# Decode states only read in the mixers and updated later on POOL; the loops over heads run one head ahead

## What is computed

```python
def step(carry, inp):                       # mLSTM, one chunk (decode: a chunk of 1)
    ...
    num = einsum('bhts,bshv->bthv', s, vc) + einsum('bht,bhvd,bthd->bthv', w_inter, cm, qc)
    den = jnp.sum(s, axis=-1) + w_inter * einsum('bhd,bthd->bht', nv, qc)
    ...
    cm_new = decay[..., None, None] * cm + einsum('bhs,bshv,bshd->bhvd', w_end, vc, kc)
    nv_new = decay[..., None] * nv + einsum('bhs,bshd->bhd', w_end, kc)

# SSD:       y = decay * cb @ x + exp(acum) * C h;   h_new = exp(acum_last) * h + w_end * x B^T
# retention: o = att @ v + w_inter * q s;            s_new = decay * s + w_end * k v^T
```

## Time and profile before

| | us |
|---|---|
| median of 3 runs | 2354.97 (2351.16 to 2358.28) |
| span of the profiled execution | 2355.1 |
| PE / DVE / ACT / POOL busy | 2187.6 / 1344.2 / 969.9 / 332.2 |
| mixers, layer 0 (first gate matmul to the squares) | 192.0 to 397.3 |
| mixers, layer 1 | 1045.5 to 1256.2 |

### The profile page before, as it was taken

One profiled execution on the slowest core, in us unless ns is written; L12 is line 12 of the kernel. 1 busy time (PEld: TensorE's weight loads), 2 busy tenths in 40 slices (PEclk: granted clock), 3 DMA queues, 4 the chain that ended last, 5 costly groups with the idle time before them and its releaser, 6 DMA issues.

```text
span 2355.1 us, 39779 instructions
## 1 busy us (share of the span) xinstructions
PE 2187.6 (93%) x16079; PEld 2027.9 (86%) x16079; DVE 1344.2 (57%) x2052; ACT 969.9 (41%) x1434; POOL 332.2 (14%) x344
## 2 busy tenths in 40 slices
PE   7998986999899999989887998899999999999997
PEld 6997765996589989988677994699999999999997
DVE  6446777541256566448676531456666666665665
ACT  4444212442155454452114441344455454454544
POOL 0872222000000004942221000000000000000000
PEclk9998888999999999998779999989999999999998
DMA  6552222454745444542222454535444544545543
GB/s 268 187 186 82 97 72 74 162 179 159 256 148 171 172 158 163 180 143 90 78 76 106 145 187 171 195 120 194 151 181 160 202 175 147 202 155 183 178 171 116
DMA packets 60747, 367.41 MB, mean 156 GB/s; under 512 B 7332, under 2 KB 7780, under 8 KB 28452
## 3 DMA queue, kind: packets, MB, share of 16 engines
q1 hardware_dynamic: 48708, 322.78, 38.8%
q0 software_dynamic: 11872, 42.28, 5.1%
HBM read 340.55 MB, written 24.48 MB: 155 GB/s over the span
## 4 chain that ended last, share of the span: by engine, by line
PE 86%; DVE 8%; ACT 3%; DMA 2%; issue 1%; SPq 0%; POOL 0%; DVEq 0%; ACTq 0%
PE ps L460 22%; PE ps L461 21%; PE ps L462 21%; PE ps L546 5%; PE ps L757 2%; PE ps L714 2%; PE ps L448 2%; PE ps L475 1%; DVE stream L1273 1%; DVE wL L309 1%; PE ps L478 1%; PE ps L738 1%; PE ps L725 1%; PE ps L477 1%; PE ps L476 1%
## 5 line engine op out<-in xcount | busy, mean ns | idle before, releaser
L309 DVE TENSOR_TENSOR wL<-ring,wH 128x1024 fp32r<-128x1024 f32 x591 | 730.2, 1237 | 508.9 <-ACT wH L303 506.7
L460 PE MATMUL ps<-hH,wH 128*128 128x264 f32 x2784 | 796.5, 286 | 19.7 <-issue 12.0
L461 PE MATMUL ps<-hL,wH 128*128 128x264 f32 x2784 | 792.4, 285 | 0.0
L462 PE MATMUL ps<-hH,wL 128*128 128x264 f32 x2784 | 791.8, 284 | 0.0
L303 ACT ACTIVATE wH<-ring 128x1024 fp32r<-128x1024 f32 x591 | 622.7, 1055 | 341.3 <-PE ps L462 265.6
L460 PEld LDWEIGHTS ps<-hH,wH 128*128 128x128 f32 x2784 | 528.2, 190 | 26.6 <-issue 22.8
L461 PEld LDWEIGHTS ps<-hL,wH 128*128 128x128 f32 x2784 | 528.4, 190 | 0.0
L462 PEld LDWEIGHTS ps<-hH,wL 128*128 128x128 f32 x2784 | 525.8, 189 | 0.0
L460 PE MATMUL ps<-projR,wH 128*128 128x264 f32 (+1 forms) x1520 | 437.7, 288 | 32.6 <-DVE projR L1353 17.3
L462 PE MATMUL ps<-projR,wL 128*128 128x264 f32 (+1 forms) x1520 | 436.7, 287 | 0.0
L461 PE MATMUL ps<-projR,wH 128*128 128x264 f32 (+1 forms) x1520 | 435.8, 287 | 0.0
(11 more groups left out here) (288 smaller groups left out, 2056.8 us busy)
## 6 DMA issues: line engine op xcount, KB each, us to landing
ring<-w_gu_dram SPq DMA_DIRECT2D x110, 1024.0 KB, 4.8
ring<-w_in_dram SPq DMA_DIRECT2D x58, 1024.0 KB, 4.7
ring<-w_down_dram SPq DMA_DIRECT2D x80, 704.0 KB, 4.1
stream<-states_dram POOLq DMA_DIRECT2D x32, 512.0 KB, 3.6
ring<-w_out_dram SPq DMA_DIRECT2D x16, 1024.0 KB, 4.7
o_states_dram<-stream POOLq DMA_DIRECT2D x32, 512.0 KB, 2.9
ring<-kc_dram SPq DMA_DIRECT2D x16, 1024.0 KB, 4.8
ring<-vc_dram SPq DMA_DIRECT2D x16, 1024.0 KB, 4.8
```

The lines of the kernel that those rows point to most:

```text
L309: dve.tensor_tensor(wL[:, buf * PIECE:(buf + 1) * PIECE], slot(s, half * PIECE, PIECE), f32(wH[:, buf * PIECE:(buf + 1) * PIECE]), ALU.sub ...
L460: pe.matmul(dst, wh, high(k0 + k), start=k0 + k == 0, stop=False)
L461: pe.matmul(dst, wh, low(k0 + k), start=False, stop=False)
L462: ins = pe.matmul(dst, wl, high(k0 + k), start=False, stop=k0 + k == k_all - 1)
```

## The change

1. **Reading.** The states are stored transposed (k x v instead of v x k, in the host's layout). `read_state(u)` on TensorE is eight matmuls with a sequence's 128x128 of the old state as weights and its q column as the one moving column; the 48 or so results of all units gather in PSUM. `spread`, `unit_half` and `decay` go. The terms with k.q come from one matmul with a block of ones (nkq), and y is finished for all heads of a kind in a few operations of 128x48 (behind mLSTM's first head, in `ssd_steps` behind the first retention head's weighing, and behind the last).
2. **Updating.** K and V (times their gates) of all units are kept in kU and vU. vU is transposed once (L671, ScalarE copies it to vT) and written to a small DRAM tensor `vrow`. When POOL has scattered the decode queries of cross attention it goes over the 16 units: load the old state again, load the unit's row of `vrow` broadcast to 128 partitions, multiply the state by its decay, the rows by k, add, write. One buffer for rows, two for states.
3. **One head ahead.** mS, mEM, mVK, mKW get two buffers (rVK, rKW in retention), the SSD tiles move to other space, products of SSD to bank 1 and 3. The loops run `a(h + 1)` before `d(h)` on TensorE, and the same on ACT and DVE.
4. **Moved.** All four rotations go ahead of the mLSTM heads. The gate activations (conv Silu, z, g, sigmoid) go from behind ACT's first two heads to ahead of them. K's scaling goes from ACT to DVE. The gate weights of layer 1 are loaded on SP behind the eighth weight block instead of at the start. `output_gate(0)` goes from unit 7 to behind unit 12.

```diff
+                def read_state(u):
+                    pe.wait_ge(state_in[u % STATE_SLOTS], 16 * state_count(l, u))
+                    S, q = state(u), unit_q(u)
+                    for b in range(NB):
+                        ins = pe.matmul(bank(u // (NH + SP), u * NB + b, 1), S[:, b * P:(b + 1) * P], q[:, b:b + 1], start=True, stop=True)
+                    ins.then_inc(dec_read, 1)
...
+                for u in range(NH):
+                    read_state(u)
+                    if u == 0:
+                        pe.wait_ge(k_scaled, l + 1)
+                    if u < RH:
+                        rotate(u)
+                pe.wait_ge(nq_ready, l + 1)
+                pe.matmul(bank(0, NQ, P), ones, nkq[:, 0:P], start=True, stop=True).then_inc(nden_ready, 1)
...
+                ml_a(0)
                 for h in range(NH):
-                    ml_a(h)
...
-                    spread(h, 0)
+                    if h + 1 < NH:
+                        ml_a(h + 1)
                     ml_d(h)
-                    spread(h, 1)
...
+                for j in range(SP):
+                    if j + 1 < SP:
+                        ssd_a(j + 1)
+                    read_state(NH + j)
+                    ssd_d(j)
+                    if j + 1 < SP:
+                        ssd_turn(j + 1)
+                pe.wait_ge(rows_ready, l + 1)
+                pe.transpose(bank(4, V_TURN, P), vU[:, :], ident).then_inc(rows_turned, 1)
...
                 for h in range(RH):
...
                     if h + 1 < RH:
+                        ret_a(h + 1)
+                    read_state(NH + SP + h)
+                    ret_d(h)
...
+                st(dve.tensor_scalar(proj[:, K_ML * NT:V_ML * NT], proj[:, K_ML * NT:V_ML * NT], P ** -0.5, None, ALU.mult))
...
+                for h in range(RH):
+                    rotate(h)
...
                 for u in range(UNITS):
-                    if u + 2 < UNITS:
-                        decay(u + 2)
-
-                    pool.wait_ge(dec_S, 2 * (l * UNITS + u + 1))
-                    pool.dma_start(t["o_states"][l, u], state(u)).then_inc(state_out[u % STATE_SLOTS], 16)
+                    pool.wait_ge(dec_read, l * UNITS + u + 1)
                     if u + STATE_SLOTS < UNITS:
-                        pool.wait_ge(state_out[u % STATE_SLOTS], 16 * state_count(l, u))
-                        pool.wait_ge(dec_read, 2 * (l * UNITS + u + 1))
                         load_state(l, u + STATE_SLOTS)
...
+                rows = stream[:, 2 * 1024:3 * 1024]
+                pool.wait_ge(rows_out, 16 * (l + 1))
+
+                def load_update(u):
+                    if u > 1:
+                        pool.wait_ge(state_out[u % 2], 16 * (l * UNITS // 2 + u // 2))
+                    pool.dma_start(stream[:, (u % 2) * 1024:(u % 2 + 1) * 1024], t["states"][l, u]).then_inc(upd_state[u % 2], 16)
...
+                for u in range(UNITS):
...
+                    if u + 1 < UNITS:
+                        load_update(u + 1)
...
+                        st(pool.tensor_tensor(S3, S3, dec.unsqueeze(2).to_broadcast([P, NB, P]), ALU.mult))
...
+                    pool.wait_ge(upd_rows, 16 * (l * UNITS + u + 1))
+                    st(pool.tensor_tensor(V3, V3, kU[:, u * NB:(u + 1) * NB].unsqueeze(2).to_broadcast([P, NB, P]), ALU.mult))
+                    st(pool.tensor_tensor(S, S, rows, ALU.add))
+                    if u + 1 < UNITS:
+                        load_rows(u + 1)
+                    pool.dma_start(t["o_states"][l, u], S).then_inc(state_out[u % 2], 16)
```

More of the change, by code:

```diff
@@ L1302, in _ @@
+                ml_weigh(0)
+                for h in range(NH):
+                    n, i = l * NH + h, h % 2
+                    if h + 1 < NH:
+                        ml_weigh(h + 1)
                     dve.wait_ge(ml_num, n + 1)
[L1303 removed]
+                    st(dve.scalar_tensor_tensor(out=mDN, in0=bank(6, SEQ, SEQ), scalar=-1.0, in1=mEM[i], op0=ALU.mult, op1=ALU.max))
@@ L1347, in _ @@
+                for h in range(RH):
+                    gamma = float(np.float32(1.0) - np.float32(2.0) ** np.float32(-5.0 - h))
+                    ins = dve.scalar_tensor_tensor(out=tile(proj, Q_R + h, SEQ, NB), in0=bank(1, 96 + h * NB, NB), scalar=gamma,
+                                                   in1=yK[:, h * NB:(h + 1) * NB], op0=ALU.mult, op1=ALU.add)
+                ins.then_inc(dec_y, 1)
                 dve.wait_ge(ret_h, (l + 1) * RH)
@@ L1591, in _ @@
+                pool.sem_inc(updated, 1)
                 pool.wait_ge(dma_out, 16 * OUTS * (l + 1))
+                for s in range(2):
+                    pool.wait_ge(state_out[s], 16 * (l + 1) * UNITS // 2)
 OUTS = 11
```

461 lines of the change are left out of this document (248 added, 213 removed).

## The result

The changed kernel takes 2405.7 us (median of 4 runs, 2399.2 to 2409.2) against 2356.1 (2351.2 to 2358.3) for the kernel before, timed beside it: a ratio of 1.0205 with a 95% interval of 1.0184 to 1.0226, slower. 2295 was forecast, 2215 to 2350 its range. The profiled execution spans 2407.0 us, 51.9 more than the one before.

A forecast was written before the change was run, and what follows sets the result against it. The tensor engine bounds nearly everything (86% of the chain that ended last). 2355.1 us, less 84 in the mixers, plus 24 for the update on POOL, gave 2295 us; range 2215 to 2350.

The forecast's parts named there:

- The share at half clock: Mixers: 40% of PE's work at half clock, so 78 - 0.4 x 91 = 42 us less a layer, 84 in all.
- its two ends: Mixers, per layer: 78 us less with PE wholly at full clock, 13 us more with it wholly at half clock.
- the prediction's own sum: Mixers of a layer at full clock: 12.6 + 40.5 + 55 + 19.5 = 127.6 us against 205.3.
- The sizes at full clock: Mixers: a read 1.5 us, mLSTM head 5.9, SSD pair 8.6, retention head 4.2; heads start 12.6 us later.
- The update: POOL from cross attention into the FFN: 11.5 us a unit, costing 12 us a layer (0 to 44), 24 in all.
- the dearer alternative: FFN: by the exclusive-lock rule each weight split could wait a whole POOL multiply, costing 10 us a layer, not 2.
- Half clock through both mixers: Rival: narrow reads and gates leave PE busy but slow in the mixers; +26 + 24, 2405 us; 10%.
- The dear lock: Rival: cross attention +20, norm +6, FFN +10, DMA +8, 44 us a layer; 2359 us, no change; 8%.
- Full clock throughout: Rival: PE waits less and holds full clock in the mixers, the whole 156 us come; 2223 us; 22%.
- Late states: Rival: PE waits for the last three of six state reads, about 3 us each, 10 a layer; 2315 us; 12%.
- The signs named for the second rival: Mixers: granted clock under 0.65 points to half clock; mixers not falling under 190 us make the forecast wrong.
- the other sign of being wrong: Forecast wrong if the stretch from 545 to 670 us grows by more than 25.

The follow-up runs named there:

- e11: Changed kernel with gate and step matmuls reading 128 rows instead of 6 or 12 (zeros added), e2 timed again in rounds: 2270.8 us, ratio 0.9641.
- e2: Changed kernel with gate and step matmuls reading 128 rows instead of 6 or 12 (added rows zeros): 2274.6 us in a single run.
- e14: Changed kernel with 128 rows in the SSD gates and steps only, mLSTM gates keeping 6 rows: 2295.8 us in a single run.
- e5: Kernel before the change, broadcasts kept, with its gate and step matmuls reading 128 rows instead of 6 or 12: 2305.0 us, ratio 0.9779.
- e4: Changed kernel with 96 unused 128x128 matmuls a layer added, at the gates and behind the first six reads: 2407.4 us in a single run.
- e10: Changed kernel with 128-row gates and update begun in the FFN, plus the six mLSTM reads moved inside the heads: 2276.4 us, ratio 0.9644.
- e9: Changed kernel with 128-row gates and the update begun only after the layer's first FFN gate-up tile: 2286.4 us, ratio 0.9698.
- e16: Changed kernel with 128-row gates, reads in mLSTM heads, eight units updated early, three beside the caches, five in the FFN: 2241.0 us, ratio 0.9494.
- e8: Changed kernel with 128-row gates and four unused 128x128 matmuls behind each of the first six reads: 2281.1 us, ratio 0.9676.
- e7: Changed kernel with the update's POOL arithmetic alone, its loads and write left out: 2395.7 us, ratio 1.0161.

## Why the prediction was wrong

**The share at half clock, the step that failed.** Between its two ends the working chose a share of 40%, "a bit higher for the missing broadcasts". The mean of 0.58 that came is a share of 84%. In the prediction's own sum 3.0 for the broadcast of the gate rows, 127.6, and 0.84 x 91 make 207 us, and 209.2 and 205.3 came. How close that is, is in part luck. e11 has means of 0.83 and 0.80, shares of 34 and 40%; the same sum gives 162 and 167 us for it, and 143.0 and 144.1 came. So at about the share that was forecast the mixers took some 20 us less a layer than the sum has for it, and what kept them from it in the changed kernel is the share alone. The row that spoke against 40% was cited: the earlier trace rows shows gates, turns and scores at 0.50 with TensorE busy throughout. What was made of it was that the clock falls sometimes. What e2, e11, e14 and e5 show is that matmuls with 6 or 12 rows pull it down: in layer 0 with the broadcasts there from 0.95 (e5) to 0.86, without them from 0.83 (e2) to 0.58. That the broadcasts had outweighed them in part, and that the change took them away, is the reading of these runs and of e4; no run puts the broadcasts themselves back. In an SSD cycle the prediction itself counted 5.9 of 8.1 us as gates, steps and reads, which should have carried the estimate to the low end.

**The sizes at full clock** can be read in e11, in the parts that run at it. An SSD pair takes 7.0 us there, 8.6 forecast; a read 1.84, 1.5 forecast. The stretch ahead of the heads takes 27, 15.6 forecast: the six reads were costed at full clock, and at half they take 3.4 each, which keeps TensorE busy for all of the stretch (15.3 us without them, e10, as forecast for VectorE). The mechanism of the change, that VectorE leaves the path and TensorE is kept fed, was right: reading and heads one ahead together are worth 39 and 40 us a layer (e5 to e2), once the clock is there.

**The update: mechanism right, size wrong.** POOL's arithmetic was forecast at 18 us and cost 45; transfers at 6 and cost 10, or 6.4 by the stage in which they show. Cross attention was taken for 5 us a layer, 1.7 for each of three heads. In layer 1 heads and units fell into step, all four heads were hit, and it cost 15.7 us there and 3.5 in layer 0, within the 0 to 20 given. The norm and the FFN had 4 us a layer, the routing of layer 1 none; 7.7 and 20.9 came. The splits L310 took 1315 ns on average where they take 1236 without the update, and L1544, with both inputs in SBUF, 523 instead of 434; L1542, with one input in PSUM, took 428 and 429. The Trainium skill (SBUF — State Buffer, Who interferes with whom) says that a VectorE instruction with two SBUF inputs contends with a GpSimd instruction that reads SBUF. The trace agrees by the numbers just given. The prediction had the splits held by this as the dearer alternative, with 10 us a layer in the FFN; e9, 20 and 38 us for sixteen units in the FFN, shows that even that was low there. A unit takes 13.4 us, not 11.5: a write now lands in 5.5 us, not 2.9, and the next load waits for it. So the update ended at 766 us instead of 730.

```profile
stream<-vrow POOLq DMA_DIRECT2D x32, 512.0 KB, 5.0
o_states_dram<-stream POOLq DMA_DIRECT2D x32, 512.0 KB, 5.5
```

**The rivals.** Half clock through both mixers had 2405 and 10%, and its mechanism is what happened; that its number was met is chance, for it had 26 us more in the mixers (1 less came) and 24 for the update (55 came). The dear lock was the other half of the truth. Taken one by one with 10 and 8%, their meeting in one execution was not considered at all. Full clock throughout did not come: in SSD TensorE was busy for 92 of 95 us at 0.50. The Trainium skill (TensorE: Matmul & The Clock Gate, What's actually happening) has the clock follow how busy TensorE has been. The trace does not agree: here that alone did not bring the full clock, and in e2 the same number of matmuls with 128-row gates got 0.83 instead of 0.58. Late states did not show: TensorE waited for no load of a state. The signs named for the second rival (clock under 0.65, mixers not under 190 us) came as written; the other sign of being wrong did not: cross attention and the caches of layer 0 grew by 8 us, not 25.

## What to carry to other kernels

Before counting what a removed matmul saves, look which matmuls hold the granted clock up. A matmul of 256 columns that used 12 of 128 rows took the same time as a full one (0.69 and 0.70 us for two) and cost the clock, and zero rows under it were free; that was worth 2.2% in the kernel before, and 5.6% in the changed one. Work moved to POOL is not free because POOL is idle. Its price was set by who waits for VectorE beside it (2276 us with all of it in the FFN, e10, and 2241 placed and paused, e16), so put it where VectorE's work is not waited for and pause it where TensorE waits for single small VectorE steps. When two risks of a change come from one cause or can come together, add them up once before setting a range.

## What the runs showed of the hardware

- The added rows hold zeros, and still the clock rose from 0.51 to 0.90 in SSD and retention of layer 0 (changed kernel to e11). It is not known from these runs why; only that rows that are read count, whatever is in them.
- One-column reads in a row ran at a low clock also with 128-row gates (the stretch ahead of the heads in e11, 0.55 with TensorE busy for all of 27.1 us), and 24 matmuls of 128 columns between them brought it to 0.84 (e8). Among full-clock work the reads did not stop it: in e11's SSD they take 1.84 us for eight. Without them the stretch is at 0.62, but TensorE then idles for a third of it (e10), so what a narrow moving operand itself does to the clock is not separated here.
- Two engines in a loop can fall into step: the head of 9.5 us and the unit of 13.4 became 13.4 and 13.4 (layer 1). With denser POOL work the heads were slow in both layers (e7, 55.7 and 55.6 us for four).
- A wait can cost more than its length, since the clock falls with it: of 18.3 us more in e7's cross attention, where the granted clock went from 1.00 to 0.80, 9.5 are TensorE busy longer with the same matmuls.
